# First projection of a pooling and convolution layer: all its weights by one queue in float32 quarters, the first 512 tokens accumulated quarter by quarter

## The chip, the cores and the metric

The kernel runs on all 8 cores of one Trainium2 chip, the same program on each, with one prompt (2048 tokens) and 16 decode sequences of 8 tokens on each. No core talks to another. The metric is the device time in microseconds of the slowest core. A core has TensorE (PE, matmuls), VectorE (DVE), ScalarE (ACT), GpSimd (POOL) and SyncE (SP); SP only issues DMAs here. Every engine works through its own list of instructions in order.

## The reference, cut to what matters

One layer, then a final norm. What the change touches is the first part: the norm, the projection on columns u, b, c and h, the pooling and the convolution.

```
hn = rmsnorm(x, g_mix)                                   # x: (tokens, 1024)
z = hn @ w_in                                            # (tokens, 4096)
u, bg, cg, hv = z[:, 0:512], z[:, 512:1024], z[:, 1024:1536], z[:, 1536:2048]
gp, gc = z[:, 2048:3072], z[:, 3072:4096]
pool_out = per-group matmul of (trailing mean over 2/4/8/16 tokens of u, minus u) * scale
conv_out = bg * conv3(cg * hv)                           # depthwise, causal, w_conv (3, 512)
merged = sigmoid(gp) * (pool_out @ w_pool_up) + sigmoid(gc) * (conv_out @ w_conv_out)
x = x + merged @ w_o
hn = rmsnorm(x, g_ffn); gu = hn @ w_ffn_in
x = x + (silu(gu[:, :2816]) * gu[:, 2816:]) @ w_ffn_out
x = x + sigmoid(rmsnorm(x, g_ple) @ w_ple_gate) * (p @ w_ple)
y = rmsnorm(x, g_final)
```

## The kernel before

Activations lie transposed in `hnT` (128 channels of each of 8 chunks x 2176 tokens, bfloat16). A token tile t is 128 tokens; there are 17. A norm of tile t has three steps: `n_a` (ACT: squares with their sum, then the root), `n_b` (the scaling, into `xn1`), `n_c` (PE transposes into a PSUM bank and one DVE copy times the gain). From tile 6 on (`TD`) there is no `n_c`: `n_b` multiplies by the gain `gmb` too, on DVE, and a DMA transpose on SP's queue writes `hnT`.

The projection works block by block of tokens (`BLK`, index `sb`): 512, 256, 256, 512, 512 and last 128. In a block, `gmm` makes one output of 128 columns: 8 matmuls over the 8 chunks into one PSUM bank, banks in turn from 8. `g_u`, `g_c`, `g_h`, `g_b` each call it for channel group 0 to 3 and evict: u by ACT, then a tree of adds on POOL and one DVE instruction (`dop`); c by ACT; h by a DVE product, then an ACT scaling and two DVE instructions (`taps`); b by a DVE product. `later` and `tick` hold work back by some outputs. The table `NS` says after which output of a block which norm step is written. Blocks 1 and 2 (256 tokens) need tiles 4 to 7, block 3 (512) needs tiles 8 to 11, all of them before its first matmul.

The weights `wres` of u, b, c and h (1024 x 2048, bfloat16) come by two roads. u and c come as float32 quarters (`wf_load`: 256 rows x 512 columns, 512 KB) on SP's queue, and ACT or DVE casts each (`wf_cast`). h and b come whole on GpSimd's queue, cast by the DMA (`wp_load`), held back by a gate until the first quarter of c is there. In block 0 the order is: u for tiles 0 and 1, u for tiles 2 and 3 (256 columns each), then c, h and b with 512 columns. The small constants come in five ACT DMAs as rows and are turned by two PE transposes. `warm(n)` issues n matmuls on the identity whose result nobody reads.

Of the kernel before, what the change touches and what calls it, by code (L numbers as in the profile page):

```python
# [165 lines left out]
def build_nc():  # L166
# [210 lines left out]
    Rwp = [Res() for _ in range(10)]; Dwp = [em.newsem("dwp%d" % i) for i in range(10)]  # L377
    Rsg = [Res() for _ in range(8)]
# [118 lines left out]
    def warm(n):  # L497
        for i in range(n):
            em.op("pe", "matmul", dict(out=psum[:, 6, 0:128], lhsT=ident[:, :], rhs=ident[:, :], start=True, stop=True),
                  reads=[Rident], writes=[Rps[6]], sig=(i == n - 1))  # L500

    warm(48)
    bq = 7
    em.op("pe", "transpose", dict(out=psum[:, bq, 0:28], in_=cst1[0:28, :], identity=identf[0:28, 0:28]),
          reads=Rrow + [Ridentf], writes=[Rps[bq]], sig=False)
    em.op("pe", "transpose", dict(out=psum[:, bq, 32:44], in_=cst2[0:12, :], identity=identf[0:12, 0:12]),
          reads=[Rrow[4], Ridentf], writes=[Rps[bq]])

    warm(16)

    def consts():
        em.op("dve", "tensor_copy", dict(out=gTall[:, 0:28], in_=psum[:, bq, 0:28]), reads=[Rps[bq]], writes=[Rg0])
        em.op("dve", "tensor_copy", dict(out=wconv[:, :, 0:3], in_=psum[:, bq, 32:44].rearrange("p (k c) -> p c k", k=3)),
              reads=[Rps[bq]], writes=[Rwc])
# [121 lines left out]
    def n_a(t):  # L636
# [9 lines left out]
        em.op("dve", "reciprocal", dict(out=rs, in_=ms), reads=[Rms], writes=[Rrs])  # L646
        return rs, Rrs
# [56 lines left out]

# [616 lines left out]
```

How the kernel before makes its waits and increments, by code:

```python
        def thunk(eng, waits=waits, fn=fn, sig=sig, s=s):  # L99
            for (ws, wv) in waits:
                eng.wait_ge(ws.h, wv)
            ins = fn(eng)
            if sig:
                ins.then_inc(s.h, 1)
# [10 lines left out]
        def thunk(eng, waits=waits, out=out, in_=in_, kw=kw, dsem=dsem):  # L115
            for (ws, wv) in waits:
                eng.wait_ge(ws.h, wv)
            eng.dma_start(out=out, in_=in_, **kw).then_inc(dsem.h, 16)
# [12 lines left out]
        def thunk(eng):  # L131
            for (s, v) in lst:
                eng.wait_ge(s.h, v)
```

## Time and profile before

| | |
|---|---|
| median of 3 runs (lowest to highest) | 990.36 us (989.82 to 991.88) |
| the profiled execution's own time | 991.43 us |
| span of its slowest core, 5 | 989.9 us |
| spans of the eight cores | 979.7 to 989.9 us |
| PE busy | 943.3 us, 95% |
| DVE, ACT, POOL busy | 450.3, 271.1, 260.8 us |
| mean granted TensorE clock, core 5 | 0.973 |

The page divides the span in 40 slices of 24.7 us. PE's busy share in tenths reads 5788799999 and then nines up to the last three: what PE idles lies in the first four or five slices. The granted clock is in tenths of 2.4 GHz, and it dips in the same slices. Time outside of the span (991.43 less 989.9) is 1.5 us.

### The profile page before, as it was taken

How to read it: one execution, taken by the hardware profiler on the slowest of the kernel's cores; microseconds unless marked ns; L12 is line 12 of the kernel's file. 1: busy time of each engine (PE TensorE's matmuls, PEld its weight loads, DVE VectorE, ACT ScalarE, POOL GpSimd, SP SyncE). 2: the span in 40 equal slices, each digit the busy share in tenths (PEclk: the TensorE clock that was granted, in tenths of full speed). 3: DMA queues.
4: the chain of work that ended last, by engine and by line, in shares of the span. 5: the costliest groups of instructions: out<-in, count | busy, mean ns of one | idle time of the engine just before them, and what ended most of it. 6: DMA issues, size and time to landing. Idle time of an engine off the chain costs nothing.

```text
span 989.9 us, 15229 instructions; the slowest of 8 cores (979.7 to 989.9 us)
## 1 busy us (share of the span) xinstructions
PE 943.3 (95%) x5034; PEld 468.2 (47%) x5034; DVE 450.3 (45%) x579; ACT 271.1 (27%) x563; POOL 260.8 (26%) x306
## 2 busy tenths in 40 slices
PE   5788799999999999999999999999999999998995
PEld 4457345654444444444444444444444444443442
DVE  2477485432222229724527324522632361264986
ACT  3345454422222214321010111011011101165543
POOL 2513246344333331011010110010310440057232
PEclk7899799999999999999999999999999999999998
DMA  8939518048342369854062244044926620036333
GB/s 253 189 100 147 114 33 75 1 52 117 35 41 27 34 142 267 176 86 43 1 75 22 20 67 42 1 67 41 129 43 85 64 45 1 1 54 123 133 134 127
DMA packets 140844, 79.36 MB, mean 80 GB/s; under 512 B 120807, under 2 KB 125583, under 8 KB 140752
## 3 DMA queue, kind: packets, MB, share of 16 engines
q0 software_dynamic: 79392, 40.44, 30.4%
q1 hardware_dynamic: 60624, 37.40, 15.4%
q8 instruction: 42, 0.69, 0.3%
q10 hardware_dynamic: 752, 0.55, 0.2%
q14 instruction: 34, 0.28, 0.1%
HBM read 87.71 MB, written 9.50 MB: 98 GB/s over the span
## 4 chain that ended last, share of the span: by engine, by line
PE 86%; DMA 4%; DVE 3%; issue 2%; POOL 2%; ACT 2%; SPq 1%; DVEq 0%; POOLq 0%; ACTq 0%
PE psum L90 86%; DVE t L90 3%; ACT t L90 2%; POOL t L90 2%; DMA t<-w_in 2%; DMA t<-t 1%; DMA t<-xp 1%; SPq L118 1%; POOL t L118 0%; DVEq L101 0%; DVEq L140 0%; ACTq L101 0%; POOLq L140 0%; POOLq L101 0%; SPq L117 0%
## 5 line engine op out<-in xcount | busy, mean ns | idle before, releaser
L90 PE MATMUL psum<-t,t 128*128 128x512 bf16 (+3 forms) x4970 | 937.5, 352 | 33.1 <-DVE t L90 14.5
L90 PEld LDWEIGHTS psum<-t,t 128*128 128x128 bf16 (+1 forms) x4970 | 462.6, 99 | 507.8 <-issue 45.4
L90 DVE TENSOR_TENSOR t<-psum,t 128x1024 f32<-128x1024 f32 (+6 forms) x381 | 314.4, 828 | 455.8 <-PE psum L90 410.9
L90 ACT ACTIVATE t<-psum 128x512 f32<-128x512 f32 (+6 forms) x296 | 152.0, 524 | 588.6 <-PE psum L90 553.7
L90 POOL TENSOR_TENSOR t<-t,t 128x1 f32<-128x1 f32 (+4 forms) x93 | 113.2, 1226 | 233.9 <-DVE t L90 166.2
L118 POOL DMA_DIRECT2D t<-w_ffn_in x44 | 38.9, 890 | 339.9 <-PE psum L90 339.5
L90 ACT ACTIVATE t<-t 128x1024 bf16<-128x1024 f32 (+5 forms) x162 | 94.0, 588 | 67.7 <-DVE t L90 56.3
L90 DVE SCALAR_TENSOR_TENSOR t<-t,t,t 128x1024 bf16<-128x1024 f32 (+4 forms) x94 | 92.4, 986 | 27.1 <-ACT t L90 12.3
L90 POOL TENSOR_TENSOR t<-t 128x512 f32<-128x512 f32 (+11 forms) x61 | 56.6, 929 | 88.8 <-ACT t L90 83.0
L90 ACT ACTIVATE t<-t,t 128x512 f32<-128x512 f32 (+3 forms) x26 | 16.6, 641 | 42.5 <-DVE t L90 42.5
L90 DVE RECIPROCAL t<-t 128x1 f32<-128x1 f32 x51 | 7.9, 156 | 38.3 <-ACT t L90 38.3
L90 DVE TENSOR_TENSOR t<-t,t 128x1024 f32<-128x1024 f32 (+3 forms) x20 | 22.8, 1139 | 2.1
L90 DVE SCALAR_TENSOR_TENSOR t<-t,t 128x512 bf16<-128x512 f32 (+2 forms) x24 | 16.8, 699 | 9.8 <-POOL t L90 6.7
L118 POOL DMA_DIRECT2D t<-xp x16 | 8.5, 542 | 34.8 <-DVE t L90 34.8
L118 POOL DMA_DIRECT2D t<-w_in x18 | 16.3, 917 | 0.4 <-issue 0.4
L90 ACT ACTIVATION_READ_ACCUMULATOR t<-t 128x1 f32 x69 | 13.1, 189 | 0.0
L90 ACT ACT_TABLE_LOAD x6 | 7.7, 1283 | 14.1 <-PE psum L90 5.8
L118 POOL DMA_DIRECT2D t<-ppr x16 | 8.6, 599 | 0.0
L90 POOL MEMSET t<- 128x1 f32 (+7 forms) x32 | 3.5, 141 | 18.4 <-DMA t<-w_in 15.6
L90 PE MATMUL psum<-t 128*128 128x128 bf16 x64 | 6.1, 282 | 1.9 <-POOL t L90 1.9
L90 PEld LDWEIGHTS psum<-t 128*128 128x128 bf16 x64 | 5.7, 133 | 1.9 <-issue 1.8
L118 POOL DMA_DIRECT2D t<-w_conv_out x8 | 6.3, 789 | 0.6 <-issue 0.3
(16 smaller groups left out, 16.8 us busy)
## 6 DMA issues: line engine op xcount, KB each, us to landing
t<-w_ffn_in POOLq DMA_DIRECT2D x44, 256.0 KB, 5.6
t<-xp SPq DMA_DIRECT2D x16, 512.0 KB, 5.9
t<-xp POOLq DMA_DIRECT2D x16, 512.0 KB, 5.7
yp<-t SPq DMA_DIRECT2D x16, 512.0 KB, 2.7
t<-w_in SPq DMA_DIRECT2D x8, 512.0 KB, 15.8
t<-w_in POOLq DMA_DIRECT2D x16, 256.0 KB, 7.2
t<-w_ffn_out POOLq DMA_DIRECT2D x4, 1024.0 KB, 11.3
t<-w_in POOLq DMA_DIRECT2D x2, 1024.0 KB, 17.0
```

Source lines behind the costliest of these rows:

```text
L90: fn = (lambda eng, meth=meth, kw=kw: getattr(eng, meth)(**kw))
L118: eng.dma_start(out=out, in_=in_, **kw).then_inc(dsem.h, 16)
```

## The change

All of the first projection's weights now come as sixteen float32 quarters on SP's queue, in the order c, h, u, b (`KIND`), each cast by ACT or DVE. Quarters of h are staged in the upper half of `hnT`, those of b in free space; tiles of x are spread among them. Block 0 takes 512 tokens at once and walks over the weights by quarters: `mmp(kind, j)` adds the two chunks of quarter j to the four banks of that kind, so 8 matmuls of 512 columns follow each quarter, and `gmm` only returns the bank for block 0. All constants come in one DMA of a prepared array (`cst`). The reciprocal of a norm moves from `n_a` to `n_b`. `NS` has new places, and the load of `w_pool_up` and the four `fuse_b` go to later ones.

```diff
-    def wp_load(i, a):
-        em.dma("pool", wres[:, :, a:a + 512], w_in[:, a:a + 512].rearrange("(k p) n -> p k n", p=128), Dwp[i], writes=[Rwp[i]])
+    KIND = "chub"
...
+    em.dma("sp", gTall[:, :], cst[:, :], Dc1, writes=[Rg0])
+    for t in range(4):
+        x_load(t)
+    for i in range(8):
+        wf_load(i)
+    x_load(4)
+    wf_load(8)
+    wf_load(9)
...
-        em.op("dve", "reciprocal", dict(out=rs, in_=ms), reads=[Rms], writes=[Rrs])
-        return rs, Rrs
+        return ms, rs, Rms, Rrs
...
+        ms, rs, Rms, Rrs = nst[t]
+        em.op("dve", "reciprocal", dict(out=rs, in_=ms), reads=[Rms], writes=[Rrs])
...
+    def mmp(kind, j):
+        for g in range(4):
+            col = UCOL[kind] + g * 128
+            b = PB0[kind] + g
+            for k in (2 * j, 2 * j + 1):
+                em.op("pe", "matmul", dict(out=psum[:, b, :], lhsT=wres[:, k, col:col + 128], rhs=hnT[:, k, 0:512],
+                                           start=(k == 0), stop=(k == 7)),
+                      reads=[wpres(kind, k)] + Rh[0:4], writes=[Rps[b]], sig=(k == 7))
...
+    n_c(0, 4)
     n_step("a", 2)
     n_step("b", 2, "dve")
+    warm(16)
+    n_c(1, 5)
     n_step("a", 3)
...
+    x_load(5)
+    for i in range(10, 16):
+        wf_load(i)
+    x_load(6)
+    x_load(7)
+    em.dma("sp", gmb[:, :], g_mix.partition_broadcast(128), Dgmb, writes=[Rgmb])
+    x_load(8)
+    warm(16)
+    n_c(2, 6)
+    warm(16)
+    n_c(3, 7)
+    warm(16)
+    wf_cast(C + 0, "act")
+    mmp("c", 0)
+    wf_cast(C + 1, "act")
+    mmp("c", 1)
...
+    wf_cast(B + 3, "act")
+    mmp("b", 3)
...
-    NS = {0: {10: "a4", 11: "b4", 12: "a5", 13: "b5", 14: "c4", 15: "c5"},
...
+    NS = {1: {0: "a6", 2: "b6", 4: "a7", 6: "b7", 8: "a8", 10: "b8", 12: "a9", 14: "b9"},
+          2: {0: "a10", 2: "b10", 4: "a11", 6: "b11", 12: "a12", 14: "b12"},
...
-            if sb == 2 and i == 0:
+            if sb == 2 and i == 10:
                 wup_load()
...
-            if sb == 3 and i in (3, 7, 11, 15):
-                fuse_b(i // 4)
+            if sb == 3 and i in (9, 11, 13, 15):
+                fuse_b((i - 9) // 2)
```

SP's queue from the start of the program: `t_93` to `t_97` are the five buffers of x, `t_80` and `t_81` the staging of u and c before, `t_78`, `t_80`, `t_79`, `t_69`/`t_83` that of c, h, u and b now, `t_79` before and `t_77` now the gain. Before:

```order
L118 DMA t_93<-xp 128x1024
L118 DMA t_94<-xp 128x1024
L118 DMA t_80<-w_in 128x2x512 x4
L118 DMA t_95<-xp 128x1024
L118 DMA t_96<-xp 128x1024
L118 DMA t_81<-w_in 128x2x512 x4
L118 DMA t_79<-g_mix 128x1024
L118 DMA t_97<-xp 128x1024
```

The same place now:

```order
L118 DMA t_59<-cst 128x48
L118 DMA t_93<-xp 128x1024
L118 DMA t_94<-xp 128x1024
L118 DMA t_95<-xp 128x1024
L118 DMA t_96<-xp 128x1024
L118 DMA t_78<-w_in 128x2x512 x4
L118 DMA t_80<-w_in 128x2x512 x4
L118 DMA t_97<-xp 128x1024
L118 DMA t_79<-w_in 128x2x512 x2
L118 DMA t_93<-xp 128x1024
L118 DMA t_79<-w_in 128x2x512 x2
L118 DMA t_69<-w_in 128x2x512 x2
```

Four tiles of x now stand ahead of the first quarter, and the quarters of h, u and b follow those of c on the same queue, with no gate between them; two more of b (`t_83`) come right behind the rows shown.

PE's list of block 0, after the first warm-up matmuls (`t_57` is the identity, `t_73` to `t_78` are buffers of normed tiles, `t_44` is `hnT`, and `t_67` before and `t_64` now are the weights). Before:

```order
L90 MATMUL psum<-t_57,t_75 128x128 x8
L90 MATMUL psum<-t_57,t_76 128x128 x8
L90 MATMUL psum<-t_44,t_67 128x256 x32
L90 MATMUL psum<-t_57,t_77 128x128 x8
L90 MATMUL psum<-t_57,t_78 128x128 x8
L90 MATMUL psum<-t_44,t_67 128x256 x32
L90 MATMUL psum<-t_44,t_67 128x512 x88
```

Now:

```order
L90 MATMUL psum<-t_57,t_75 128x128 x8
L90 MATMUL psum<-t_57 128x128 x16
L90 MATMUL psum<-t_57,t_76 128x128 x8
L90 MATMUL psum<-t_57 128x128 x16
L90 MATMUL psum<-t_44,t_64 128x512 x88
L90 MATMUL psum<-t_57,t_73 128x128 x8
L90 MATMUL psum<-t_44,t_64 128x512 x16
L90 MATMUL psum<-t_57,t_74 128x128 x8
L90 MATMUL psum<-t_44,t_64 128x512 x24
```

The 64 matmuls of 256 columns for u became 32 of 512; warm-up matmuls stand between the tiles' transposes; and the first matmul on weights now waits for all four tiles.

DVE's list in the middle of block 2, one channel group (`t_69` before and `t_66` now are the product c times h, `t_83` and `t_82` the convolution, `t_46` is `conv_out`, `t_45` `pool_out`, and the instruction on 1024 elements is a norm's scaling). Before:

```order
L90 TENSOR_TENSOR t_69<-psum,t_83 128x256
L90 RECIPROCAL t_65<-t_65 128x1
L90 SCALAR_TENSOR_TENSOR t_83<-t_69,t_62,t_83 128x256 x2
L90 TENSOR_TENSOR t_46<-psum,t_83 128x256
L90 SCALAR_TENSOR_TENSOR t_45<-t_82,t_68 128x256
L90 SCALAR_TENSOR_TENSOR t_77<-t_93,t_65,t_79 128x1024
```

Now:

```order
L90 TENSOR_TENSOR t_66<-psum,t_82 128x256
L90 RECIPROCAL t_62<-t_62 128x1
L90 SCALAR_TENSOR_TENSOR t_75<-t_93,t_62,t_77 128x1024
L90 SCALAR_TENSOR_TENSOR t_82<-t_66,t_59,t_82 128x256 x2
L90 TENSOR_TENSOR t_46<-psum,t_82 128x256
L90 SCALAR_TENSOR_TENSOR t_45<-t_81,t_65 128x256
```

The norm's scaling now stands right behind the h product and its own reciprocal, ahead of the taps; before, the reciprocal stood there alone, and its `n_a` stood behind the h product's ACT scaling in ACT's list.

## Rows read from the trace of the kernel before

**Rows 1.** Spans and clock by core: two of eight cores.
```profile
core 5: 989.9 us, clock 0.973
core 6: 988.1 us, clock 0.974
```

**Rows 2.** PE's timeline of core 5 from 105 us: start, duration, work, [idle before].
```profile
105.78 261.01 PE L90 MATMUL psum<-t,t 128*128 128x512 bf16 x1444 [8.61 <-DMA t<-t]
368.80 540.36 PE L90 MATMUL psum<-t,t 128*128 128x512 bf16 x2756 [2.00 <-DVE t L90]
911.74 66.60 PE L90 MATMUL psum<-t,t 128*128 128x512 bf16 x300 [2.58 <-ACT t L90]
```

**Rows 3.** PE's timeline of core 5 before 105 us.
```profile
32.29 24.19 PE L90 MATMUL psum<-t,t 128*128 128x256 bf16 x120 [1.48 <-DVE t L90]
...
63.29 24.71 PE L90 MATMUL psum<-t,t 128*128 128x256 bf16 x212 [2.09 <-DVE t L90]
90.10 7.07 PE L90 MATMUL psum<-t,t 128*128 128x256 bf16 x48 [2.10 <-DVE t L90]
```

**Rows 4.** PE's timeline of core 6: block 1's and block 3's first matmul.
```profile
64.39 24.66 PE L90 MATMUL psum<-t,t 128*128 128x256 bf16 x212 [2.09 <-DVE t L90]
...
103.33 21.96 PE L90 MATMUL psum<-t,t 128*128 128x512 bf16 x90 [5.09 <-DMA t<-t]
```

**Rows 5.** Windows of 3 us, core 5: busy PE, PEld, DVE, ACT, POOL, clock, DMA share, GB/s.
```profile
15.00:18.00 3.00, 0.80 (x7) 0.45 (x6) 1.75 (x2) 1.06 (x1) 0.00 (x0) 1.00 1.02 309
18.00:21.00 3.00, 1.63 (x9) 1.02 (x8) 0.69 (x1) 0.39 (x1) 0.00 (x0) 0.57 1.01 324
...
24.00:27.00 3.00, 1.32 (x7) 0.59 (x4) 0.00 (x0) 1.59 (x5) 1.75 (x2) 0.79 0.51 85
...
39.00:42.00 3.00, 3.00 (x15) 1.37 (x14) 1.58 (x1) 1.20 (x2) 2.57 (x4) 1.00 1.05 264
```

**Rows 6.** Timeline of core 5: first instruction released by each landed transfer.
```profile
5.01 1.06 ACT L90 ACTIVATE t<-t 128x1024 bf16<-128x1024 f32 x1 [0.26 <-DMA t<-xp]
...
16.66 1.06 ACT L90 ACTIVATE t<-t 128x1024 bf16<-128x1024 f32 x1 [2.23 <-DMA t<-w_in]
...
23.23 0.10 POOL L90 MEMSET t<- 128x1 f32 x1 [15.59 <-DMA t<-w_in]
...
27.05 0.34 SPq L118 DMA_DIRECT2D t<-g_mix  x1
```

**Rows 7.** Timeline of core 5: two of ACT's copies from PSUM in block 0.
```profile
41.04 0.60 ACT L90 ACTIVATE t<-psum 128x512 f32<-128x512 f32 x1 [1.02 <-PE psum L90]
42.76 0.60 ACT L90 ACTIVATE t<-psum 128x512 f32<-128x512 f32 x1 [1.13 <-PE psum L90]
```

**Rows 8.** Timeline of core 5: DVE in block 2, h product to h product.
```profile
84.94 0.42 DVE L90 TENSOR_TENSOR t<-psum,t 128x256 f32<-128x256 f32 x1
...
87.46 0.16 DVE L90 RECIPROCAL t<-t 128x1 f32<-128x1 f32 x1 [2.10 <-ACT t L90]
...
91.39 0.42 DVE L90 TENSOR_TENSOR t<-psum,t 128x256 f32<-128x256 f32 x1
```

**Rows 9.** DVE's groups by form, core 5, 66 to 105 us: busy, mean ns.
```profile
L90 DVE SCALAR_TENSOR_TENSOR t<-t,t,t 128x256 f32<-128x256 f32 x16 | 9.7, 609 | 4.6 <-ACT t L90 3.8
L90 DVE SCALAR_TENSOR_TENSOR t<-t,t,t 128x1024 bf16<-128x1024 f32 x6 | 8.4, 1398 | 0.1
...
L90 DVE RECIPROCAL t<-t 128x1 f32<-128x1 f32 x6 | 1.0, 161 | 8.1 <-ACT t L90 8.1
```

**Rows 10.** DMAs of core 5 in the first 260 us: total, and us to landing.
```profile
DMA packets 36486, 27.27 MB, mean 105 GB/s; under 512 B 27511, under 2 KB 30111, under 8 KB 36448
...
t<-w_pool_up POOLq DMA_DIRECT2D x1, 1024.0 KB, 13.5
...
t<-t SPq DMA_TRANSPOSE x11, 3.6
```

**Rows 11.** SP's timeline of core 5: the last DMA transpose ahead of block 3.
```profile
97.96 4.04 SPq L118 DMA_TRANSPOSE t<-t  x1
```

More of the change, by code:

```diff
@@ L376, in build_nc @@
     Rctm = Res(); Rctv = Res()
-    Rwp = [Res() for _ in range(10)]; Dwp = [em.newsem("dwp%d" % i) for i in range(10)]
-    Rsg = [Res() for _ in range(8)]
+    Rwp = [Res() for _ in range(16)]; Dwp = [em.newsem("dwp%d" % i) for i in range(16)]
+    Rsg = [Res() for _ in range(16)]
     Rwup = Res(); Dwup = em.newsem("dwup")
@@ L498, in warm @@
         for i in range(n):
[L499 to L514, printed above, removed]
+            em.op("pe", "matmul", dict(out=psum[:, 0, 0:128], lhsT=ident[:, :], rhs=ident[:, :], start=True, stop=True),
+                  reads=[Rident], writes=[Rps[0]], sig=(i == n - 1))
+    warm(64)
+    mk_ident(identf, Ridentf)
     wins = [2, 4, 8, 16]
@@ new lines, in build_nc @@
+    wf_cast(C + 1, "act")
+    mmp("c", 1)
+    wf_cast(C + 2, "dve")
+    mmp("c", 2)
+    wf_cast(C + 3, "dve")
+    mmp("c", 3)
+    for r_ in Rwn + Rcs:
+        r_.inherit(*Rsg[C:C + 4])
+    wf_cast(H + 0, "act")
+    for cc in range(4):
+        g_c(cc, 0)
+    wf_cast(H + 1, "dve")
+    mmp("h", 0)
+    mmp("h", 1)
+    wf_cast(H + 2, "dve")
+    mmp("h", 2)
+    wf_cast(H + 3, "dve")
+    mmp("h", 3)
+    for t in range(8, 16):
+        Rh[t].inherit(*Rsg[H:H + 4])
+    wf_cast(U + 0, "dve")
@@ L883, in build_nc @@
+    for g in range(4):
+        g_h(g, 0)
+    mmp("u", 0)
+    wf_cast(U + 1, "dve")
+    mmp("u", 1)
+    n_step("a", 4)
+    pop()
+    wf_cast(U + 2, "dve")
+    mmp("u", 2)
+    n_step("b", 4, "act")
+    pop()
+    n_step("a", 5)
+    wf_cast(U + 3, "dve")
+    n_c(4, 7)
+    mmp("u", 3)
+    n_step("b", 5, "act")
+    wf_cast(B + 0, "dve")
+    mmp("b", 0)
     for g in range(4):
         for tb in range(5):
-            Rco[g][tb].inherit(*Rsg[4:8])
+            Rco[g][tb].inherit(*Rsg[U:U + 4])
@@ L886, in build_nc @@
+    for g in range(4):
+        g_u(g, 0)
+    pop()
+    n_c(5, 0)
+    wf_cast(B + 1, "act")
+    mmp("b", 1)
+    pop()
+    wf_cast(B + 2, "dve")
+    mmp("b", 2)
+    pop()
+    wf_cast(B + 3, "act")
+    mmp("b", 3)
+    pop()
+    d2, d3 = later.pop(0)[1], later.pop(0)[1]
+    for r_ in Rwf + [Rwup]:
+        r_.inherit(*Rsg[B:B + 4])
+    for cc in range(4):
+        g_b(cc, 0)
+    assert not later
+    later.extend([[3, d2], [8, d3]])
+    bankc[0] = 0
     em.dma("act", wgf[:, :, :], w_pg.rearrange("g c d -> c g d"), Dmisc, writes=[Rwgf])
@@ L944, in run_sb @@
                 w_issue()
-    for sb in range(LB):
+    for sb in range(1, LB):
         run_sb(sb)
@@ L1288, with lay_cst @@
 _NC_CACHE = {}
+def lay_cst(gm, gf, gp, ps, wc):
+    c = np.zeros((128, 48), dtype=np.float32)
+    for i, v in enumerate((gm, gf, gp)):
+        c[:, 8 * i:8 * i + 8] = v.reshape(8, 128).T
+    c[:, 24:28] = ps.reshape(4, 128).T
+    c[:, 32:48].reshape(128, 4, 4)[:, :, 0:3] = wc.reshape(3, 4, 128).transpose(2, 1, 0)
+    return c
 def kernel(x_prompt, x_sample, state_pool, state_conv, p_prompt, p_sample,
```

125 lines of the change are left out of this document (48 added, 77 removed), and 4 rows, old and new, of the table NS.

## The prediction

> **What bounds the kernel now.** I read the clock and spans by core first: the spans differ by 10 us, and cores 5 and 6 end last [rows 1]. Then PE's timeline. From 105.78 us on core 5's PE stops twice, for 2.0 and 2.58 us, up to 978 us [rows 2], so about 884.1 us of the span (989.9 less 105.78) are a run of matmuls with almost nothing to win. All that the change can touch lies before block 3's first matmul, at 105.78 us on core 5 and 103.33 us on core 6 [rows 2, 4]. The rest after that point is 884.1 and 884.8 us (988.1 less 103.33).
>
> How much of these 105.8 us is needed? At full clock one output of 8 matmuls with 512 columns takes 1.72 us (42.76 less 41.04) [rows 7]. Block 0 has 16 of them, 27.5 us; blocks 1 and 2 have together the same, 27.5 us. So 55 us of matmuls take 105.8. Three stretches hold the loss. (a) Up to 32.3 us: the matmuls work in pieces behind weights and norms, and the clock is 0.57 in 18 to 21 us [rows 3, 5]. (b) Block 0 runs from 32.29 to 56.5 and block 1 starts at 63.29 [rows 3]. (c) Blocks 1 and 2 take 63.29 to 97.17, and then PE waits 8.61 us for a DMA transpose [rows 2, 3].
>
> What paces (c) is DVE: from one h product to the next it took 6.45 us (84.94 to 91.39), of which it stood 2.10 us before a reciprocal that waits for ACT [rows 8]. The six reciprocals of the stretch waited 8.1 us together [rows 9].
>
> **The change: loading.** Transfers of 512 KB on SP's queue land, counted from the first: the 1st at 5.01 us, the 5th at 16.66, the 9th at 23.23, the 12th at 27.05 [rows 6]. At 15 to 21 us 309 to 324 GB/s are moved; at 24 to 27 the queue has run dry and it is 85 [rows 5]. In the new order x0 to x3 are the 1st to 4th, c0 to c3 the 5th to 8th, h the 9th to 12th, then x4, u0, u1, x5, u2, u3, b0 to b3: b3 is the 22nd. The constants' array ahead of them is 24 KB, nothing here. Past the 12th the price of a transfer is between 1.66 us (0.524 MB at 316 GB/s) and 2.0 us ((27.05 less 5.01)/11); I take the middle, 1.83. b3 then lands at 27.05 + 10 x 1.83 = 45.4 us (43.7 to 47.1).
>
> By the Trainium skill ("DMA: Bandwidth & Descriptors", section "Bandwidth") HBM gives a core about 358 GB/s when its neighbour streams too; by that a transfer would take 1.46 us and b3 land at 41.7. The trace shows no more than 324 over 3 us.
>
> **The change: block 0.** Tile x3 is the 4th transfer, about 13.4 us. Its square takes 1.06 us [rows 6], with the root, reciprocal, scaling on ACT (about 1.1, the same size), transposes and copy about 5 us in all: the first matmul on c0 starts at about 18.4, c0's cast being done at 17.7. PE then needs 1.72 us a quarter against 1.3 to 2.0 of delivery: c3 ends at 25.3, h3 at 32.1, about with the delivery. u waits a little: u1's cast stands on DVE behind four h products of 0.7 us, so u0 to u3 end at about 33.8, 36.6, 38.9, 41.4. Two tiles' transposes are 1.2 us. b1's cast stands on ACT behind four copies of 0.6 us (to 43.8) and takes 1.06: b0 to b3 end at 43.4, 46.7, 48.6 and 50.3. Block 1 can start there: **50.5 us** where it was 63.29. If the clock is at its lower level for the first 4 us of weights, PE loses 2 us that it had spare anyway, about 1 us at the end. Bounds: 48 (delivery at 1.66, 1.1 for the cast, 1.7 for the matmuls, and no DVE wait) to 56 (each of the eight DVE casts of u and b late by another 0.7 us). The warm-up matmuls and the removed GpSimd loads cost nothing: PE would wait for x3 anyway.
>
> **Blocks 1 and 2.** DVE's work for a channel group is the h product 0.42 [rows 8], the b product and dop on the same 256 elements as much each, two taps 1.2, reciprocal 0.16, norm 1.4 [rows 9]: 4.0 us, and the norm now covers ACT's scaling, so that no wait is left but small ones: 4.2 a group. DVE first finishes block 0's four b products (52.5), so block 1's first h product is at 53. The two dops held over from block 0, with their small companions, add 1.9. Tile 11's scaling stands behind the h product of block 2's second group: 53 + 5 x 4.2 + 1.9 + 0.42 + 0.16 + 1.4 = 77.9. Its transpose took 3.6 us in the median; the last one before, issued at 97.96 [rows 11] and landed at 105.7, took 7.7, beside the load of w_pool_up (13.5 us to landing) [rows 10], which now starts only behind it. I take the median: 81.5. PE reaches the end of block 2 at about 81 by then (it runs at most eight banks ahead of DVE), so the wait for the transpose is under 1 us. **Block 3 starts at 81.5** (77 with groups of 3.8 and block 1 at 48; 86 with a 7.7 us transpose).
>
> w_pool_up is wanted at block 3's tenth output, 15.5 us behind its start, and is issued about 4 us before its start: 19.5 us for a load of 13.5. It costs nothing; were it 6 us slower, PE would stand for that.
>
> **The sum.** Core 6, the longer rest: 81.5 + 884.8 = 966.3. After the waits of 8.6 and 5.1 us the clock came back at its lower level; without such a wait about 4 us of matmuls run twice as fast, 2 us less: 964.3. Outside of the span 1.5: 965.8. The profiled execution (991.43) was 1.1 above the median (990.36): 964.7, say **965 us**, 2.6% less.
>
> **The rivals.**
> - *Only the head start counts.* Blocks 1 and 2 stay as slow as before, because what DVE no longer waits before a reciprocal it waits elsewhere, or the transposes stay late. From 50.5 core 6 needs its old 38.9 (103.33 less 64.39), core 5 its 42.5: block 3 at 89.4 to 93.0, the run at 974 to 977. For it: DVE waits for ACT before the taps too, 3.8 us in 16 [rows 9]. Against: these lie in groups in which no norm covered them. 0.16.
> - *Better in everything.* Delivery at 1.66, groups of 3.8 us, no late transpose: block 3 at 74 to 77, 957 to 961. 0.12.
> - *The clock stays low in block 0.* Every quarter ends with PE short of weights, so that its clock falls again each time: 16 quarters of 3.44 us from 18.4 and the two transposes end at 74.6, block 3 is at about 105.6, 989 us: no change. The trace speaks against: in the unbroken run from 32.29 us the clock was 1.00 at 39 to 42, and at 15 to 18 it stood at 1.00 though PE was 27% busy [rows 3, 5]; and a PE at half clock is slower than the delivery, so it never stops, which is what raised the clock. 0.03. The Trainium skill has this rule: "TensorE: Matmul & The Clock Gate", section "HAM oscillation — how this bites in real kernels", says that a loop over K tiles whose matmuls are shorter than the wait for the next weights falls to half clock every time. By that rule this rival's time would come; the trace's waits of a few tenths per quarter are too short for it.
> - *The queue starves (slower).* One queue carries 8 MB of float32 weights that all of block 0 waits for. If from the 12th transfer on it gave only the 105 GB/s that is the mean of the first 260 us [rows 10], 5.0 us a transfer, b3 would land at 77, block 1 start at 80, block 3 at 111: about 995 us. It decides from 4.5 us a transfer on (116 GB/s), where block 3 is at 106. Against: 309 to 324 GB/s at 15 to 21 us [rows 5]. 0.03.
> - In between, a late cast or a late gain array that costs 10 to 20 us: 978 to 987. 0.04.
>
> **How the numbers follow.** The forecast (block 3 at 77 to 86, 961 to 970) has 0.62. The cases faster than before add to 0.62 + 0.16 + 0.12 + 0.04 = 0.94; no change 0.03; slower 0.03. A difference under 0.2%, 2 us, is about what a measurement of this kernel can't tell from none. The range, 958 to 977, takes in the forecast, the head-start rival and most of the better one; the forecast's own is 961 to 970.
>
> **What would show it.** In the changed profile: the first 512-column matmul on weights at 18 to 19 us; block 1's first matmul of 256 columns at 48 to 53; DMA at about 310 GB/s until 40 us; DVE's reciprocals without waits in blocks 1 and 2, and 4.2 us from h product to h product; block 3's first matmul at 77 to 86 with under 2 us of wait for a transpose; from there 880 to 885 us to the end. The prediction is wrong if the quarters land slower than 2.0 us each, if DVE's casts hold PE in u and b, or if PE comes to stand in the part from block 3 on (for w_pool_up at its tenth output, for a tile's transpose in block 4), which the rows before show nearly without a wait.

## The result, and the profile after

The changed kernel takes **977.76 us** (median of 4 runs, 977.65 to 978.25), the kernel before 990.36 (median of 3, 989.82 to 991.88). The ratio is 0.987 (95% interval 0.9851 to 0.989): 1.3% less time, where 965 us (2.6% less) was forecast and 977 was the end of the range. Executions in which the clock of a whole die was visibly disturbed are left out in all that follows. The profiled execution took 978.25 us, with a span of 976.7.

The spans and clocks of three cores after (before: [rows 1]; there the clock was 0.973 to 0.979), and then from the page PE's busy time, busy tenths and clock in 40 slices:

```profile
core 5: 975.3 us, clock 0.992
core 6: 970.5 us, clock 0.992
core 7: 976.7 us, clock 0.992
```

```profile
PE 938.4 (96%) x5064; PEld 463.5 (47%) x5064; DVE 456.5 (47%) x586; ACT 270.1 (28%) x560; POOL 258.5 (26%) x303
...
PE   7787999999999989999999999999999999998995
...
PEclk9999999999999999999999999999999999999998
```

PE idles some 38 us: 22 in the first four slices (98 us), where the change works, 11 in the last 77 us, which the change leaves alone (before, core 5 idled 14 of its last 90 us), and 5 between. The clock is nearly full in the first four slices too (0.98). Core 7 ends last. Its PE timeline (start, duration, work, idle before) answers to [rows 3] and [rows 4]:

```profile
18.09 3.61 PE L90 MATMUL psum<-t,t 128*128 128x512 bf16 x16 [0.58 <-DVE t L90]
...
36.77 1.89 PE L90 MATMUL psum<-t,t 128*128 128x512 bf16 x8 [0.72 <-DVE t L90]
...
54.02 16.71 PE L90 MATMUL psum<-t,t 128*128 128x512 bf16 x136 [1.96 <-DVE t L90]
...
84.20 5.40 PE L90 MATMUL psum<-t,t 128*128 128x256 bf16 x48 [0.17 <-DVE t L90]
93.87 18.32 PE L90 MATMUL psum<-t,t 128*128 128x512 bf16 x78 [4.26 <-DMA t<-t]
```

The weights' matmuls start at 18.09, as forecast (18.4). u0's quarter starts at 36.77 (forecast 33.8 less 1.7, so 32.1), b2's at 54.02 (46.9), block 3 at 93.87 (81.5). From there core 7 needs 882.8 us more, just what the sum had (884.8 less 2). So the whole miss, 12.4 us, lies before block 3. That the rest fits so exactly is luck. The 884.8 was core 6's, and core 6 needs 879.5 now; the mean of the cores went from 882.4 to 880.2. And the 2 us were to come from a clock that no longer falls ahead of block 3, but it did fall (1.00 is 2.4 GHz, 0.50 is 1.2 GHz). Windows of 3 us as in [rows 5], core 7:

```profile
93.00:96.00 3.00, 2.13 (x6) 0.77 (x7) 2.79 (x5) 0.03 (x1) 1.31 (x1) 0.53 1.09 284
```

PE had stood still for 4.26 us just before. On all eight cores it waited 2.7 to 5.5 us there, and on all eight the clock then fell in the same way.

The table gives the marks that all experiments are read by. Each is the start of a row in the timelines (DVE's cast of quarter u0 and of b2, DVE's first b product of block 0, its first h product of block 1, PE's first matmul of block 3), as the mean over the eight cores of the profiled execution; "rest" is the mean from there to the end of the span.

| kernel | cast u0 | cast b2 | b product | h product | block 3 | rest | ratio to before (95%) |
|---|---|---|---|---|---|---|---|
| before | – | – | 58.2 | 68.1 | 102.7 | 882.4 | 1 |
| changed kernel | 35.3 | 51.6 | 58.2 | 61.0 | 93.0 | 880.2 | 0.987 (0.9851–0.989) |
| e1_no_tree0 | 35.2 | 50.8 | 54.1 | 58.5 | 90.0 | 880.7 | 0.9871 (0.9795–0.9946) |
| e2_order | 35.1 | 47.9 | 53.1 | 63.2 | 95.1 | 879.9 | 0.9884 (0.9825–0.9944) |
| e3_spool_late | 35.4 | 51.8 | 58.3 | 61.2 | 90.8 | 878.9 | 0.983 (0.977–0.9891) |
| e4_gate3 | 32.2 | 48.7 | 55.3 | 58.1 | 89.7 | 879.4 | 0.9843 (0.9778–0.9908) |
| e5_load_only | 35.4 | 55.1 | 61.7 | 66.0 | 100.4 | 880.3 | 0.998, two runs |
| e6_table_only | – | – | 57.6 | 66.7 | 96.0 | 880.6 | 0.992 (0.9895–0.9945) |
| e7_u_first | – | 51.9 | 58.1 | 60.7 | 90.5 | 881.8 | 0.9865 (0.9845–0.9886) |
| e9_all3 | – | 48.7 | 55.0 | 57.6 | 83.5–84.1* | 881.3* | 0.9783 (0.9766–0.98) |
| e10_recip_back | – | 55.5 | 62.2 | 66.2 | 96.9 | – | 0.9921 (0.9905–0.9936) |
| e11_wup_early | – | 52.5 | 59.0 | 61.8 | 98.6 | – | 0.9934 (0.9909–0.9959) |
| e12_gate2 | – | 52.3 | 58.6 | 61.3 | 86.3–87.9* | – | 0.9851 (0.983–0.9872) |

(*) On the cores where PE stops right before block 3 (0, 2, 3 and 7 in e9, 2 and 3 in e12); on the others its matmuls run on. Over all cores block 3 starts at 83.2 in e9 and 87.4 in e12. A dash: the row isn't there or not on every core, the quarter has another place (u0 in e7 and e9), or (rest of e10 to e12) it isn't compared. e1 to e4, e5 to e9 and e10 to e12 ran on three different chips. On the first two the kernel before took 990.9 and 990.4 us. On the third it took 998.4, and there the granted clock also stood at 0.81 for long stretches (on two cores of e12 from 93 to 105 us), which no other trace here shows up to 105 us; so only ratios and marks are compared with e10 to e12, and the marks behind some 63 us with care. The runs of the kernel before beside e1 to e4 scattered (989.47 to 1001.51), hence the wide intervals; the marks decide there.

### The profile page after: what moved, and what is told of

It reads as the page before. It is cut to its first block, busy times and chain, and to the rows that moved or that the text cites. A ratio compares the mean times of both kernels' runs of the same rounds, so it can differ in the third digit from the quotient of the medians.

```text
span 976.7 us, 15297 instructions; the slowest of 8 cores (970.1 to 976.7 us)
## 1 busy us (share of the span) xinstructions
PE 938.4 (96%) x5064; PEld 463.5 (47%) x5064; DVE 456.5 (47%) x586; ACT 270.1 (28%) x560; POOL 258.5 (26%) x303
## 4 chain that ended last, share of the span: by engine, by line
PE 87%; DMA 4%; SPq 3%; DVE 2%; issue 2%; ACT 1%; POOL 1%; DVEq 0%; POOLq 0%; ACTq 0%
PE psum L90 87%; SPq L118 3%; DVE t L90 2%; DMA t<-w_in 2%; DMA t<-xp 1%; ACT t L90 1%; DMA t<-t 1%; POOL t L90 1%; POOL t L118 0%; DVEq L140 0%; DVEq L101 0%; POOLq L140 0%; ACTq L101 0%; POOLq L101 0%; SPq L117 0%
## 5 line engine op out<-in xcount | busy, mean ns | idle before, releaser
L90 PE MATMUL psum<-t,t 128*128 128x512 bf16 (+2 forms) x4936 | 928.3, 350 | 25.2 <-DVE t L90 16.2
L90 PEld LDWEIGHTS psum<-t,t 128*128 128x128 bf16 x4936 | 453.5, 98 | 499.6 <-issue 39.0
L90 ACT ACTIVATE t<-psum 128x512 f32<-128x512 f32 (+6 forms) x292 | 150.0, 528 | 566.3 <-PE psum L90 537.2
L90 DVE TENSOR_TENSOR t<-t,t 128x1024 f32<-128x1024 f32 (+3 forms) x22 | 24.8, 1125 | 2.3
L118 POOL DMA_DIRECT2D t<-xp x16 | 8.5, 540 | 35.3 <-DVE t L90 35.3
L90 DVE CAST t<-t 128x1024 bf16<-128x1024 f32 x11 | 8.4, 768 | 15.2 <-DMA t<-w_in 15.2
L118 POOL DMA_DIRECT2D t<-w_in x16 | 14.3, 907 | 0.0
L90 PE MATMUL psum<-t 128*128 128x128 bf16 x128 | 10.8, 260 | 1.8 <-POOL t L90 1.8
L90 PEld LDWEIGHTS psum<-t 128*128 128x128 bf16 x128 | 10.2, 121 | 1.8 <-issue 1.8
## 6 DMA issues: line engine op xcount, KB each, us to landing
t<-w_in SPq DMA_DIRECT2D x16, 512.0 KB, 17.7
```

The lines of the kernel that those rows point to most:

```text
L90: fn = (lambda eng, meth=meth, kw=kw: getattr(eng, meth)(**kw))
L118: eng.dma_start(out=out, in_=in_, **kw).then_inc(dsem.h, 16)
```

## The experiments

### Which half of the change brought what: e5 and e6

e5 has the loading of the changed kernel and everything else as before. Its diff against the changed kernel:

```
-    NS = {1: {0: "a6", 2: "b6", 4: "a7", 6: "b7", 8: "a8", ...
+    NS = {1: {0: "a6", 1: "b6", 3: "a7", 4: "b7", 8: "a8", ...     # the places of before
     # in n_a, behind the root:
+        em.op("dve", "reciprocal", dict(out=rs, in_=ms), reads=[Rms], writes=[Rrs])
     # in n_b:
-        em.op("dve", "reciprocal", dict(out=rs, in_=ms), reads=[Rms], writes=[Rrs])
-            if sb == 2 and i == 10:
+            if sb == 2 and i == 0:
                 wup_load()
-            if sb == 3 and i in (9, 11, 13, 15):
+            if sb == 3 and i in (3, 7, 11, 15):
```

> The changed kernel with the loading and block 0 of the change, but the norm steps' places, the reciprocal in n_a, the load of w_pool_up and the fuse_b as before. As mean over the cores block 3 starts at 102.7 us before and at 93.0 in the changed kernel. If the two halves of the change add: block 1's first h product at 61 as in the changed kernel, then 6.4 us a group in block 2 again and a transpose of 6 to 8 us beside w_pool_up: block 3 at 96 to 98, the run 5 to 7 us under before. If the head start were all: block 3 at 93 to 94.

e6 is the kernel before with the other half: the places of the norms in blocks 1 to 3, the reciprocal in n_b, wup_load at output 10, fuse_b at 9 to 15 (the same lines the other way round).

> The kernel before with only the other half: reciprocal in n_b, the new places of the norm steps, of w_pool_up's load and of fuse_b. If the halves add: block 1 starts where it did (first h product 68.2 us in the mean), block 2's groups take 3.8 to 4.3 us instead of 6.4, block 3 starts at 98 to 99 instead of 102.7, the run 3 to 5 us under before. If what DVE no longer waits before reciprocals is lost elsewhere: block 3 within 1 us of 102.7 and the run the same.

Measured: e5 988.08 and 988.7 us against 990.44, e6 983.34 (0.992). Block 3 starts 2.3 us earlier than before in e5, 6.7 in e6, 9.7 with both: the halves nearly add up. My sum had given the loading 13 us by itself; in e5 the first h product comes only 2.1 us earlier than before. A part of that lies in e5's other edit, as e10 below shows: the reciprocal in n_a delays block 0 by some 5 us. With the old table block 2 goes at its old pace. DVE on core 7 in e5, which answers to [rows 8]:

```profile
81.64 0.42 DVE L90 TENSOR_TENSOR t<-psum,t 128x256 f32<-128x256 f32 x1
84.15 0.16 DVE L90 RECIPROCAL t<-t 128x1 f32<-128x1 f32 x1 [2.09 <-ACT t L90]
...
87.73 0.42 DVE L90 TENSOR_TENSOR t<-psum,t 128x256 f32<-128x256 f32 x1
```

and the same stretch in the changed kernel:

```profile
80.48 0.42 DVE L90 TENSOR_TENSOR t<-psum,t 128x256 f32<-128x256 f32 x1
80.82 0.15 DVE L90 RECIPROCAL t<-t 128x1 f32<-128x1 f32 x1
...
84.31 0.42 DVE L90 TENSOR_TENSOR t<-psum,t 128x256 f32<-128x256 f32 x1
```

6.09 us from h product to h product and a wait of 2.09, against 3.83 and none.

That is one group, though. From block 1's first h product to block 2's second it took 22.8 us on the mean before and 22.7 in the changed kernel: what block 2's groups save, block 1's lose, because the changed kernel holds two dops of block 0 over into block 1 (its first two groups take 4.9 and 5.7 us there, 4.3 and 3.5 before). In e6, which has the new places without that, the same stretch takes 19.6.

### The reciprocal's place in block 0: e10

The changed kernel with one line back in n_a (and out of n_b):

```
         em.op("act", "activation", dict(out=ms, in_=ms, func=AF.Sqrt, ...
+        em.op("dve", "reciprocal", dict(out=rs, in_=ms), reads=[Rms], writes=[Rrs])
         return ms, rs, Rms, Rrs
```

> The changed kernel with only the reciprocal of a norm moved back into n_a, where DVE meets it before ACT has its sum of squares. If that move carries the second half's gain: groups of block 2 cost DVE up to 2 us more for each norm whose n_a stands right ahead, and in block 0 the casts of u2 to b2 wait too (the load-only kernel had 3 to 4 us there): first h product of block 1 at 63 to 66 in the mean instead of 61.0, block 3 at 96 to 99 instead of 93.0. If the new places in the table carry it (n_b now two outputs behind n_a): block 3 within 1 us of 93.0.

Ratio 0.9921 against 0.987. b2's cast comes at 55.5 in place of 51.6 and the first h product at 66.2 in place of 61.0: in block 0 the reciprocal holds up the casts of the weights that stand behind it on DVE (on core 7 it waits 2.02 us for ACT ahead of u2's cast, and PE then waits 2.45 us). From then on, h product to block 3, e10 needs 30.7 us and the changed kernel 32.0, so in blocks 1 and 2 the new places suffice without the move. The two edits of the table half work in different places: the reciprocal's in block 0, the places' in blocks 1 and 2.

### GpSimd's additions at the end of block 0: e1 and e2

In the changed kernel block 0's window sums (11 additions on GpSimd) come at the very end of the block, beside DVE's last work. Core 7, all engines (there is no such stretch before, where the additions lay earlier, at 35 to 48 us):

```profile
48.08 14.02 POOL L90 TENSOR_TENSOR t<-t 128x512 f32<-128x512 f32 x11 [40.94 <-DVE t L90]
...
50.21 2.19 DVE L90 SCALAR_TENSOR_TENSOR t<-t,t,t 128x512 f32<-128x512 f32 x2
52.33 1.55 DVE L90 CAST t<-t 128x1024 bf16<-128x1024 f32 x1
53.79 2.99 DVE L90 SCALAR_TENSOR_TENSOR t<-t,t 128x512 bf16<-128x512 f32 x2
...
56.89 2.07 DVE L90 TENSOR_TENSOR t<-t,t 128x32 f32<-128x32 f32 x2
58.88 2.47 DVE L90 TENSOR_TENSOR t<-psum,t 128x512 bf16<-128x512 f32 x4
59.05 0.21 ACT L90 ACTIVATE t<-t 128x15 f32<-128x15 f32 x1 [7.90 <-DVE t L90]
...
61.55 0.42 DVE L90 TENSOR_TENSOR t<-psum,t 128x256 f32<-128x256 f32 x1 [0.19 <-ACT t L90]
```

e1 leaves block 0's additions out (its dops then read u where they would read the sums):

```
         if last:
-            tree(g, sb)
+            if sb > 0:
+                tree(g, sb)
```

> Leaves out the GpSimd adds of the pooling for the first 512 tokens (the two or three DVE instructions that read their result read u instead; block 0's pooling output is therefore other). Theory A, that DVE's instructions at the end of block 0 are stretched by the GpSimd adds beside them: DVE's pair of taps goes back from 2.19 to 1.6 us, the cast of b2 from 1.55 to 0.7, the two dops from 2.99 to 1.4, the two small ones from 2.07 to 0.4; DVE's first b product comes 4 us earlier (58.9 to 55), block 3 starts 3 to 4.5 us earlier, the run is 3 to 4.5 us shorter than the changed kernel's. Rival B, that only the order of DVE's and ACT's lists and the landing of the quarters hold the end of block 0: these durations stay, and the run is within 1 us.

The same four groups of DVE in e1, core 7, and its first h product:

```profile
47.62 1.60 DVE L90 SCALAR_TENSOR_TENSOR t<-t,t,t 128x512 f32<-128x512 f32 x2
...
49.13 0.69 DVE L90 CAST t<-t 128x1024 bf16<-128x1024 f32 x1
49.73 1.29 DVE L90 SCALAR_TENSOR_TENSOR t<-t 128x512 bf16<-128x512 f32 x2
...
51.13 0.49 DVE L90 TENSOR_TENSOR t<-t,t 128x32 f32<-128x32 f32 x2
...
52.39 2.48 DVE L90 TENSOR_TENSOR t<-psum,t 128x512 bf16<-128x512 f32 x4 [0.77 <-PE psum L90]
...
56.78 0.43 DVE L90 TENSOR_TENSOR t<-psum,t 128x256 f32<-128x256 f32 x1 [1.91 <-ACT t L90]
```

4.07 us of work became 8.80 beside GpSimd. Even an operation on 32 elements goes from 0.25 to 1.03 us. The cast, the dops and this small one each become 0.8 to 0.9 us longer, whatever their own length, and one GpSimd addition takes 1.27 us (14.02/11). That speaks for a wait for the other's instruction and against a shared rate. The four b products, which take one of their inputs from PSUM, stay the same beside the additions (2.47 and 2.48 us). The Trainium skill ("SBUF — State Buffer", section "Who interferes with whom") says that a DVE operation with two SBUF inputs, and a copy or cast in a two-port mode, takes turns with GpSimd, instruction by instruction; the trace agrees. The kernel before had the same in two of its dops beside its additions (core 5):

```profile
36.31 0.69 DVE L90 SCALAR_TENSOR_TENSOR t<-t,t 128x512 bf16<-128x512 f32 x1 [2.96 <-ACT t L90]
39.28 1.58 DVE L90 SCALAR_TENSOR_TENSOR t<-t,t 128x512 bf16<-128x512 f32 x1 [2.27 <-POOL t L90]
```

On the mean of the cores the first h product comes 2.5 us earlier in e1 and block 3 3.0 us. The run doesn't follow (978.64): the span averaged over cores and executions fell from 972.7 to 971.7 only, and the slowest core is as late as ever. More on this below.

e2 keeps the additions, and moves the casts of b1 and b2 ahead of other work and the first two dops behind the b products:

```
+    wf_cast(B + 1, "act")
     for g in range(4):
         g_u(g, 0)
     pop()
+    wf_cast(B + 2, "dve")
     n_c(5, 0)
-    wf_cast(B + 1, "act")
     mmp("b", 1)
...
     for cc in range(4):
         g_b(cc, 0)
+    d0()
+    d1()
```

> Only the order at the end of block 0 is other: ACT casts b1 ahead of its four copies of u, DVE casts b2 ahead of a tile's copy and a pair of taps, and the first two dops stand behind the four b products. Theory B (order): b1's matmuls start 2 us earlier, b2's 3 us earlier, block 1's first matmul at about 54 instead of 57.5, DVE's first h product of block 1 3 to 4 us earlier, the run 3 to 4 us shorter. Theory A (stretching alone): the same DVE work beside the same adds, the run within 1.5 us. Theory C (the quarters land too late): b2's cast would wait for its quarter, and less than 1.5 us is won.

e2 took 980.98 us (980.66 to 982.26), 3 more than the changed kernel. The b products came 5 us earlier and the first h product 2 us later. Core 7:

```profile
51.59 2.48 DVE L90 TENSOR_TENSOR t<-psum,t 128x512 bf16<-128x512 f32 x4 [0.24 <-PE psum L90]
54.00 2.68 DVE L90 SCALAR_TENSOR_TENSOR t<-t,t 128x512 bf16<-128x512 f32 x2
56.78 2.06 DVE L90 TENSOR_TENSOR t<-t,t 128x32 f32<-128x32 f32 x2
58.94 0.21 ACT L90 ACTIVATE t<-t 128x15 f32<-128x15 f32 x1 [9.67 <-DVE t L90]
```

ACT's small copy of u's history (15 columns) has to wait until the dop and its correction of the first 16 columns have read u. It stands first on ACT's queue for block 1, and behind it the copies that free PSUM. So the last b product, which my 50.5 took, isn't all that opens block 1: there is also the chain additions, dop, history copy. In the changed kernel the two end together: the h product waits 0.2 us for ACT behind the b products, on seven of eight cores. e2 brought only the first chain forward. The second, with the dops behind the b products, became longer: on the mean the history copy starts at 60.7, where it was 58.4, and the h product waits 2.58 us for ACT on every core.

### The pace of landings: e4 and e12

DMA in windows of 3 us on core 7 (columns as in [rows 5]), and the start of DVE's casts there:

```profile
18.00:21.00 3.00, 2.92 (x14) 1.39 (x15) 0.00 (x0) 0.93 (x1) 0.00 (x0) 1.00 0.98 295
21.00:24.00 3.00, 2.46 (x12) 0.81 (x9) 0.81 (x2) 0.00 (x0) 0.00 (x0) 1.00 0.96 315
24.00:27.00 3.00, 2.40 (x12) 1.10 (x12) 0.58 (x1) 1.88 (x3) 0.00 (x0) 1.00 0.98 330
27.00:30.00 3.00, 2.20 (x12) 0.81 (x10) 0.69 (x1) 1.13 (x3) 0.00 (x0) 1.00 0.99 359
30.00:33.00 3.00, 1.81 (x9) 0.71 (x8) 0.69 (x1) 0.00 (x0) 0.00 (x0) 1.00 0.91 275
```

```profile
21.39 0.69 DVE L90 CAST t<-t 128x1024 bf16<-128x1024 f32 x1 [3.45 <-DMA t<-w_in]
...
28.30 0.69 DVE L90 CAST t<-t 128x1024 bf16<-128x1024 f32 x1 [3.72 <-DMA t<-w_in]
...
33.31 0.69 DVE L90 CAST t<-t 128x1024 bf16<-128x1024 f32 x1 [1.25 <-DMA t<-w_in]
```

The bytes flow as forecast: 4.72 MB in these 15 us ((295 + 315 + 330 + 359 + 275) x 3), nine transfers' worth, 1.67 us each. But from c2, the 7th transfer, cast at 21.39, to h3, the 12th, cast at 33.31, one lands every 2.4 us. Eight or nine of these transfers were under way at a time, and one took 17.7 us in the median from its issue to its landing. Before, the 12th landed at 27.05 [rows 6] with nothing queued behind it. The explanation to test: the DMA engines that are ahead already work on later transfers, and a transfer has landed only when the last of its pieces has. e4 lets a weights' transfer start only when the one three places ahead has landed:

```
+        gate = Res()
+        if i >= 3:
+            gate.w = list(Rsg[i - 3].w)
         em.dma("sp", stg_of(i), ...,
-               Dwp[i], writes=[Rsg[i]])
+               Dwp[i], reads=[gate], writes=[Rsg[i]])
```

> SP issues a quarter of weights only when the third quarter before it has landed, so that at most three are under way. Theory D, that the faster of the 16 DMA engines run ahead into later transfers and take bandwidth from the slowest, which sets each landing (2.2 us apart, where the bytes would allow 1.7): landings come at about 1.75 us, u3's cast no later than 39 instead of 44.0, the run 2 to 4 us shorter. Rival E, that the slowest engine has this pace by itself: landings stay at 2.2 us or get later by the round trip of each gate, and the run is 0 to 4 us longer.

The casts of c2, h3 and u0 on core 7 in e4:

```profile
18.31 0.69 DVE L90 CAST t<-t 128x1024 bf16<-128x1024 f32 x1
...
30.05 0.69 DVE L90 CAST t<-t 128x1024 bf16<-128x1024 f32 x1 [2.70 <-DMA t<-w_in]
33.82 0.69 DVE L90 CAST t<-t 128x1024 bf16<-128x1024 f32 x1 [3.07 <-DMA t<-w_in]
```

Means over the cores: c2 17.8 in place of 21.1, h3 29.1 for 32.8, u0 32.2 for 35.3, block 3 89.7 for 93.0; the median run 976.52. The median time of a quarter from issue to landing is 6.8 us on core 7. A shorter queue delivers each piece sooner, though not more bytes. The median run gained 1.2 us and not 2 to 4, and u3's cast came at 41.1 and not at 39: from u0's cast on DVE works without waiting for a quarter up to u3, so there its own list sets the pace. The gate holds only quarters of weights; with tiles of x up to five transfers were under way up to u3's issue. e12 (the kernel e9, below, with 2 in place of 3) asks how short:

> The best kernel so far (u first, at most three quarters under way, state loads late; 968.9 us) with at most two under way. If a shallow queue is all that the slowest DMA engine needs: quarters land as early or earlier, block 3 within 1 us of 83.5. If the round trip of the gate then leaves the engines idle: the rate falls under 280 GB/s in 15 to 30 us, u2 to h3 are cast 1 to 4 us later, and the run is 1 to 4 us longer.

Too short, as the rival said: 143 to 225 GB/s in the windows of 3 us from 15 to 30 us on core 7 and 194 to 261 on core 0, b2's cast at 52.3 and the b product at 58.6, where e9 has 48.7 and 55.0, ratio 0.9851 against 0.9783 (on another chip).

### The last transpose: e3 and e11

Block 3's first matmul waits for tile 11's transposed values. SP's queue on core 7 of the changed kernel:

```profile
85.33 0.91 SPq L118 DMA_DIRECT2D t<-spool  x2
...
86.29 0.40 SPq L118 DMA_DIRECT2D t<-sconv  x1
...
86.80 1.26 SPq L118 DMA_TRANSPOSE t<-t  x1
```

Issued at 86.80, it let PE go at 93.87: 7.1 us, of which my sum had 3.6. On the mean of the cores it landed 6.2 us after its issue (5.0 to 7.8). Loads for the last stage (480 and 64 KB) are issued right ahead, and a tile of x (512 KB) ahead of these. e3 moves them behind:

```
-            if sb == 2 and i == 2:
+            if sb == 2 and i == 8:
                 for h_ in range(2):          # the loads of spool and sconv
```

> The loads of the pooling and convolution states go from block 2's third output to its ninth, behind the DMA transpose of tile 11 in SP's queue. Theory: that transpose, 7.1 us from issue to PE's start, then takes its median 3.1 to 3.6, block 3 starts at about 90.3 instead of 93.9, and the run is 3 to 4 us shorter. Rival: the transpose is late from x's loads and the wait of its own queue, not from these: 0 to 1 us. Second rival: what is won ahead of block 3 is lost again in it, because DVE is then eight banks behind: under 1 us in the end.

```profile
87.67 1.23 SPq L118 DMA_TRANSPOSE t<-t  x1
...
89.56 1.20 SPq L118 DMA_DIRECT2D t<-spool  x2
```

The transpose now goes first (above: core 7 of e3), and block 3 starts at 90.8 in place of 93.0 with the same first h product (61.2 for 61.0); the run takes 975.34. The transpose lands 4.5 us after its issue on the mean, not 3.1 to 3.6. On core 7 it takes 5.3 us and is issued later, so that block 3 starts at 93.25 there, hardly earlier. From block 2's second h product to block 3 it is 6.8 us on the mean, where it was 9.3. The opposite, w_pool_up's load back at block 2's start:

```
-            if sb == 2 and i == 10:
+            if sb == 2 and i == 0:
                 wup_load()
```

> The changed kernel with only the load of w_pool_up back at block 2's first output. If that load beside the transposes of tiles 8 to 11 costs what I ascribed to it: tile 11's transpose lands 1 to 3 us later, block 3 at 94 to 96 in the mean instead of 93.0, the run 1 to 3 us longer. If only SP's own loads matter for the transposes: the same within 1 us.

Core 7 of e11:

```profile
91.91 3.37 SPq L118 DMA_TRANSPOSE t<-t  x1
```

```profile
100.88 11.32 PE L90 MATMUL psum<-t,t 128*128 128x512 bf16 x41 [9.49 <-DMA t<-t]
```

PE waits 9.49 us (7.5 to 9.7 on the eight cores), block 3 comes at 98.6, more than the 94 to 96 that I expected, the ratio is 0.9934: about half of the change's gain is gone by this one place.

### Other orders and the best version: e7 and e9

e7 takes the columns in the order u, c, h, b, so that GpSimd's additions run while c and h are loaded, and the dops come before the h products:

```
-    KIND = "chub"
+    KIND = "uchb"
-    PB0 = {"c": 0, "h": 4, "u": 0, "b": 4}
+    PB0 = {"u": 0, "c": 4, "h": 0, "b": 4}
...
     # behind the casts of b, ahead of block 1:
-    d2, d3 = later.pop(0)[1], later.pop(0)[1]
+    for i in range(3):
+        pop()
...
-    later.extend([[3, d2], [8, d3]])
```

> The changed kernel with the kinds in the order u, c, h, b, so that GpSimd's 14 us of adds run beside the loading of c and h and not beside the end of block 0, and the dops stand ahead of the h products. Theory A (the adds stretch DVE's instructions and hold block 1's first u, which waits for the second dop): DVE's taps of block 0 take 1.6 us a pair, ACT's history copy of block 1 no longer waits for a dop, the first h product of block 1 comes at 57 to 59 instead of 61.0 in the mean, block 3 at 89 to 91 instead of 93.0, the run 2 to 4 us shorter. Rival: the casts of c and h are stretched in their place (1.5 us each instead of 0.7) and PE loses that: no change.

Block 3 is 2.5 us earlier on the mean and the run the same, 977.65: on cores 3, 5 and 7 the rest was 884.8 to 885.3, on the others 879.6 to 880.2. The gain isn't the expected one. The first h product doesn't come earlier (60.7 for 61.0), because the additions now stretch casts of c and h (to between 0.96 and 1.74 us on core 7), as the rival said. What is won is the two held-over dops, which no longer lie in block 1: from its first h product to block 2's second it takes 20.0 us in place of 22.7.

e9 is e7 with e4's gate and e3's late loads.

> u first, at most three quarters under way, and the state loads behind tile 11's transpose, all in one. If the three gains (about 3, 3.3 and 2.3 us at block 3's start in the mean) add: block 3 at 84 to 86, the run 969 to 972 us. If u first and the gate remove the same wait (PE then bound by DVE's chain from u0's cast on): 87 to 88 and 972 to 974.

It took **968.91 us** against 990.44 for the kernel before (968.17 to 970.26), ratio 0.9783; the changed kernel's 977.76 is 8.9 us more, at a ratio of 0.987. PE on core 7, and its windows as above:

```profile
83.50 28.86 PE L90 MATMUL psum<-t,t 128*128 128x512 bf16 x133 [0.24 <-DMA t<-t]
```

```profile
83.00:86.00 3.00, 2.75 (x15) 1.20 (x13) 2.60 (x6) 2.18 (x8) 2.55 (x4) 1.00 0.90 261
```

With the three edits block 3 starts at 83.5, 10.4 us sooner than on core 7 of the changed kernel, in the interval of 77 to 86 that was forecast for the change itself. Tile 11's transpose lands 3.4 us after its issue on the mean, and PE, which waits for it at most 1.4 us, keeps its clock there on all eight cores. The sum isn't confirmed by that, since it had the two dops in block 1 and e9 hasn't.

## Why the prediction was wrong, step by step

**Right.** Where the time could come from: all before block 3, and 882.8 us from there on. The start of the weights' matmuls (18.09, forecast 18.4). The reciprocals without waits (none in 60 to 95 us on core 7) and the pace of blocks 1 and 2: on the mean 22.7 us from block 1's first h product to block 2's second, forecast 5 x 4.2 + 1.9 = 22.9; but the kernel before took 22.8 for the same stretch, so that here nothing was won, which the sum didn't say. The price of a transfer past the 12th: landings at 32.7 and 49.1 us for the 12th and the 22nd on the mean, 1.64 each. w_pool_up's late load cost nothing: from 93.87 us on, PE of core 7 runs 259.8 us without a stop. The clock in block 0: 1.00 in every window of 3 us from 18 to 90 us on seven of the eight cores, though PE waited 0.2 to 2.0 us at nearly every quarter. On core 4 it fell once, behind waits of 1.21 and 1.96 us with 1.89 us of matmuls between them:

```profile
54.00:57.00 3.00, 3.00 (x9) 1.10 (x8) 2.79 (x4) 0.00 (x0) 2.86 (x3) 0.52 0.05 20
```

So the rival "the clock stays low in block 0" fell for this kernel, but the waits were not far from those that bring the clock down: in e5, where every core waited 2.46 us ahead of u2's matmuls, it fell behind that wait on six of the eight (to 0.53 in 45 to 48 us on core 5). The Trainium skill's rule behind it ("TensorE: Matmul & The Clock Gate", section "HAM oscillation — how this bites in real kernels"), a fall at every K tile, did not come: the trace of core 7 has none in block 0.

**Wrong: three terms before block 3.** On the means of the cores block 3 starts at 93.0 where I had 81.5, 11.5 us late:

1. *"Past the 12th the price of a transfer is between 1.66 and 2.0 us", counted from h3 at 27.05.* h3 was cast at 32.8. u0's matmuls started at about 36.3 (cast at 35.3, plus the 1.0 that core 7 took from 35.81 to 36.77) against 32.1: **+4.2 us**. The rate was right; the landing time was read from a queue with nothing behind the 12th. e4 shows that it is the number of transfers under way that does it (h3's cast 3.7 us sooner).
2. *"DVE first finishes block 0's four b products, so block 1's first h product is at 53."* It came at 61.0, 8.0 late, 3.8 more than by the first point. GpSimd's additions beside DVE make 2.5 of it (e1), and e2 shows that the h product waits for the history copy behind the additions as well as for the b products. **Of the other 1.3**, 0.8 can be put down to DVE's own chain from cast u0 to cast b2: 15.6 us in e1, where 14.8 was forecast from u0's start to b2's; 0.5 stays open. That DVE's casts would hold PE in u and b was one of the signs of being wrong that the prediction named, and it came: at each u quarter and at b2 PE of core 7 waits for DVE (0.2 to 2.0 us). My part on the change never asked when block 0's additions run. The profile of before had the hint in its two-input operations on DVE (0.69 and 1.58 us, above); no row of it stands in my list.
3. *"I take the median", 3.6 us for tile 11's transpose.* It took 7.1 on core 7. From block 2's second h product (83.7) to block 3 it was 9.3 us against 5.6: **+3.7**. I knew of a transpose of 7.7 us [rows 10, 11] and put it down to w_pool_up's load alone. Both loads do it (e3, e11); the small ones now stand right ahead of the transpose. Moving them gives 2.5 of the 3.7 back (e3: 6.8 us); in e9 the stretch takes the 5.6 of the forecast.

4.2 + 3.8 − 0.2 + 3.7 = 11.5, and core 7 has 0.9 more. The total then follows: 976.7 of span, 1.5 around it.

**The rival that came closest in time** was "only the head start counts", 974 to 977. It wasn't right either, but it was nearer than the forecast. Block 3 came 9.7 us earlier: 7.1 by the head start (first h product 68.1 to 61.0), which was to be 13; nothing from there to block 2's second h product (22.8 and 22.7), as that rival said; and 2.5 from there to block 3 (11.7 and 9.3), where it said nothing. The range ended where that rival did; the bound of a 7.7 us transpose and that of a late delivery were each given (block 3 at 86; b3 at 47.1), but never together, nor the 27.05 itself any bound.

**What stays open.** An earlier block 3 doesn't always shorten the run: e1 and e7 start it 2.5 to 3.0 us earlier on the mean, and their medians are those of the changed kernel. In pairs of neighbouring cores (0 and 1, 2 and 3, and so on) the one that reaches block 3 later needed more time from there in 30 of 36 pairs (the nine kernels up to e7; in the changed kernel itself in 2 of 4), 881.8 us on the mean against 879.1, with a wait of PE for DVE of up to 2.7 us at about 350 to 370 us, where the next stage's tiles are loaded. That neighbours compete for the loads there would fit; so would, for a part, the clock that falls behind the longer waits ahead of block 3. No run tested either.

## What to carry to other kernels

Read a landing time only together with what was queued behind it: a deep queue keeps its rate and delays each single landing, and at most three quarters of weights under way were here better than all (and than two). When DVE moves onto the path, look which of its operations would then run beside GpSimd's, and count them at the length of GpSimd's. A DMA transpose that PE waits for goes ahead of small loads on the same queue and away from big ones; taking its median is taking the case without them.

## What the runs showed of the hardware

- 128-partition additions on GpSimd (1.27 us each) made DVE operations on SBUF beside them longer by 0.8 to 0.9 us, less than one addition: 32 elements 0.25 to 1.03 us, a cast of 1024 elements 0.69 to 1.55, a two-input operation on 512 elements 0.65 to 1.50. Operations with one input in PSUM stayed the same (four in 2.47 and 2.48 us).
- With eight or nine transfers of 512 KB under way, one landed every 2.4 us from the 7th to the 12th while 1.67 us' worth of bytes was moved; with at most three quarters under way the 12th was cast 3.7 us sooner.
- The DMA transpose of tile 11 landed 3.4 us after its issue in e9 and 6.2 behind 544 KB of loads, on the mean of the cores, and PE waited up to 9.7 us for one beside a load of 1 MB.
- PE's clock stayed at 1.00 on seven of eight cores from 18 to 90 us, with waits of 0.2 to 2.0 us at nearly every quarter. It fell to 0.5 on all eight behind the wait of 2.7 to 5.5 us ahead of block 3, and on none in e9, where that wait was at most 1.4 us.
